# Attention bias tables loaded from ScalarE's queue in a two-layer streaming encoder

## The reference, cut to what matters

```python
x = x + 0.5 * swiglu(rmsnorm(x, g0), w_gu, w_down)
y = even_mixer(...) if l % 2 == 0 else odd_mixer(...)   # one layer each
x = x + y
x = x + 0.5 * swiglu(rmsnorm(x, g2), w_gu, w_down)
```

```python
s = einsum('bihd,bjhd->bhij', q, k) * D ** -0.5
s = s + bias                             # band: by distance, from a table
s = s + F_q[..., :, None] - F_k[..., None, :]   # fox: cumulative log forget values
p = softmax(s); o = einsum('bhij,bjhd->bihd', p, v)
```

## Time and profile before

| what | value |
|---|---|
| runs | 2955.0, 2948.9, 2955.4 us; median 2955.0 us |
| profiled execution | span of 2944.9 us from the first to the last instruction |
| TensorE matmul busy | 2773.1 us, 94% of the span |
| mean granted TensorE clock | 0.968 |
| VectorE, ScalarE, GpSimd busy | 25%, 24%, 32% |
| transfers | 293.49 MB, mean 100 GB/s |

### The profile page before, as it was taken

The page is one execution under the profiler, slowest core; times in us unless marked ns, Lnnn a source line. Parts: engine busy times, 40 slices in busy tenths (PEclk is TensorE's granted clock), DMA queues, the critical chain, the costliest instruction groups (busy, mean ns, idle before and its releaser), DMA issues.

```text
span 2944.9 us, 48416 instructions
## 1 busy us (share of the span) xinstructions
PE 2773.1 (94%) x19827; PEld 2646.2 (90%) x19827; DVE 739.6 (25%) x1751; ACT 708.7 (24%) x973; POOL 944.0 (32%) x285
## 2 busy tenths in 40 slices
PE   7999999999779999999999999999777789999997
PEld 7999999998548999999999999999545579999997
DVE  4110114323543211112211012311234433110112
ACT  2221222210242222122222122211244432221221
POOL 3443444330003344344344344432000013443442
PEclk9999999996699999999999999999899999999998
DMA  3212212112242221221221221222677832212211
GB/s 130 71 68 89 72 59 85 64 51 95 100 175 75 72 82 65 82 71 63 92 75 67 78 73 61 93 87 91 236 269 279 286 135 72 71 68 85 76 53 69
DMA packets 52873, 293.49 MB, mean 100 GB/s; under 512 B 8065, under 2 KB 11922, under 8 KB 28722
## 3 DMA queue, kind: packets, MB, share of 16 engines
q1 hardware_dynamic: 52786, 292.24, 28.1%
HBM read 279.95 MB, written 12.27 MB: 99 GB/s over the span
## 4 chain that ended last, share of the span: by engine, by line
PE 85%; DMA 5%; issue 4%; DVE 3%; ACT 1%; POOL 0%; SPq 0%; DVEq 0%; ACTq 0%
PE ps L306 75%; DMA s_bias<-neg_f_dram 4%; PE ps L670 4%; PE ps L932 1%; PE ps L984 0%; PE ps L922 0%; PE ps L1274 0%; DMA p_bias<-neg_f_dram 0%; DVE xn_lo L407 0%; PE ps L1263 0%; PE ps L372 0%; PE ps L1249 0%; PE ps L1269 0%; PE ps L912 0%; POOL w_lo L292 0%
## 5 line engine op out<-in xcount | busy, mean ns | idle before, releaser
L292 POOL TENSOR_TENSOR w_lo<-w_raw,w_hi 128x2048 fp32r<-128x2048 f32 (+2 forms) x185 | 791.7, 4279 | 1132.5 <-ACT w_hi L287 1124.2
L306 PE MATMUL ps<-xn_hi,w_hi 128*128 128x320 f32 x3616 | 829.8, 311 | 19.1 <-POOL w_lo L1641 10.9
L306 PE MATMUL ps<-xn_lo,w_hi 128*128 128x320 f32 x3616 | 827.4, 310 | 0.0
L306 PE MATMUL ps<-xn_hi,w_lo 128*128 128x320 f32 x3616 | 826.3, 310 | 0.0
L306 PEld LDWEIGHTS ps<-xn_hi,w_hi 128*128 128x128 f32 x3616 | 606.9, 189 | 21.6 <-POOL w_lo L1641 10.9
L306 PEld LDWEIGHTS ps<-xn_lo,w_hi 128*128 128x128 f32 x3616 | 607.8, 189 | 0.0
L306 PEld LDWEIGHTS ps<-xn_hi,w_lo 128*128 128x128 f32 x3616 | 607.6, 189 | 0.0
L287 ACT ACTIVATE w_hi<-w_raw 128x2048 fp32r<-128x2048 f32 (+2 forms) x185 | 326.6, 1766 | 533.5 <-PE ps L306 444.1
L559 POOL TENSOR_TENSOR h_lo<-prod,h_hi 128x640 f32 x88 | 139.1, 1581 | 716.5 <-ACT h_hi L512 716.5
L306 PE MATMUL ps<-h_hi,w_hi 128*128 128x320 f32 x1408 | 320.9, 309 | 0.0
L306 PE MATMUL ps<-h_hi,w_lo 128*128 128x320 f32 x1408 | 320.8, 309 | 0.0
(11 more groups left out here) (187 smaller groups left out, 2073.9 us busy)
## 6 DMA issues: line engine op xcount, KB each, us to landing
w_raw<-in_w_up SPq DMA_DIRECT2D x87, 1024.0 KB, 4.7
k_cache<-in_fox_kc SPq DMA_DIRECT2D x16, 2048.0 KB, 13.6
v_cache<-in_fox_vc SPq DMA_DIRECT2D x32, 1024.0 KB, 9.2
w_raw<-in_w_down_a SPq DMA_DIRECT2D x32, 768.0 KB, 4.3
w_raw<-in_w_in SPq DMA_DIRECT2D x24, 1024.0 KB, 4.7
w_raw<-in_w_down_b SPq DMA_DIRECT2D x32, 640.0 KB, 3.8
k_cache<-in_band_kc SPq DMA_DIRECT2D x8, 1024.0 KB, 7.0
v_cache<-in_band_vc SPq DMA_DIRECT2D x8, 1024.0 KB, 5.8
```

Of the source, the lines that this page charges most:

```text
L292: nc.gpsimd.tensor_tensor(out=w_lo[:, slot, 0:cols], in0=w_raw[:, slot, 0:cols], in1=w_hi[:, slot, 0:cols].bitcast(F32), op=ALU.subtract). ...
L306: last = nc.tensor.matmul(ps[:, 2 * unit + half, 0:HALF], w_part[:, slot, w:w + P], a_part[:, k, half * HALF:(half + 1) * HALF], start=k = ...
```

## The change

The bias loads of both stages are issued from ScalarE's queue. The pieces B (prompt bias, one head) and sB (sample bias, one unit) are put into ACT_HEAD and ACT_ORDER, each behind the exp that had to wait for the maximum that frees the tile, so they have no wait of their own. SyncE's order loses them with their waits; the rest of it is as it was. ScalarE waits for the end of GLA ahead of band. The data, the tiles and the semaphores that the loads raise are the same.

```diff
-    ACT_HEAD = "Q E0 E1 sE0".split()
+    ACT_HEAD = "sB0 B0 B1 Q E0 E1 sE0 sB1".split()
...
-    ACT_ORDER = ("C0 E2 sC0a sC0b sC0c C1 E3 C2 H0 E4 sE1 C3 E5 sH0 C4 H1 E6 sC1a sC1b sC1c C5 E7 Q+ C6 W H2 sE0+ "
-                 "C7 E0+ E1+ sH1 H3").split()
+    ACT_ORDER = ("C0 E2 sC0a sC0b sC0c C1 E3 C2 H0 E4 sE1 sB0+ C3 E5 sH0 C4 H1 E6 B0+ sC1a sC1b sC1c C5 E7 B1+ Q+ C6 W H2 "
+                 "sE0+ sB1+ C7 E0+ E1+ sH1 H3").split()
...
-                def bias(u):
-                    if not first or u:
-                        sp.wait_ge(self.smax_step, i * 4 + 2 * u)
-                    loads["bias"](i, u)
-
-                def prompt_bias():
-                    for hh in range(2):
-                        wait(self.max_step, i * 16 + (2 * hh - 2))
-                        sp.dma_start(p_bias[:, hh, :], self.prompt_bias(i, hh)).then_inc(self.bias_loaded[hh], 16)
...
+            def prompt_bias(i, hh):
+                act.dma_start(p_bias[:, hh, :], self.prompt_bias(i, hh)).then_inc(self.bias_loaded[hh], 16)
+
+            def sample_bias(i, u):
+                load_bias(i, u)
...
+    def fox_bias(act):
+        def load(i, u):
+            act.dma_start(s_bias[:, 0:PAST], after_dram[bass.ds(i * H_C + 8 * u, 8), :].unsqueeze(1)
+                          .broadcast_to([8, DEC_SEQ, PAST])).then_inc(fox.sbias_loaded[u], 16)
+            act.dma_start(s_bias[:, PAST:PAST + P], neg_f_dram[8 * u:8 * u + 8, SEQ:T].unsqueeze(1)
+                          .broadcast_to([8, DEC_SEQ, P])).then_inc(fox.sbias_loaded[u], 16)
+        return load
...
+                act.wait_ge(g_olo, H_A)
+                band.act(act, lambda: out_first(act, ph, band), band_bias(act))
...
+                fox.act(act, lambda: out_first(act, ph, fox), fox_bias(act))
```

More of the change, by code:

```diff
@@ L771, in out_dve @@
                 acc_dve(dve, s, u, (KT * r, SQ_STEPS * r))
-    PE_HEAD, DVE_HEAD, ACT_HEAD = "S0 S1 sS0".split(), "sQ0 sQ1 M0 M1 sM0".split(), "Q E0 E1 sE0".split()
+    PE_HEAD, DVE_HEAD, ACT_HEAD = "S0 S1 sS0".split(), "sQ0 sQ1 M0 M1 sM0".split(), "sB0 B0 B1 Q E0 E1 sE0 sB1".split()
     PE_ORDER = ("T0 S2 sT0a sT0b sT0c V0 sV0a T1 S3 V1 sV0b sS1 T2 X0 S4 V2 sV0c T3 S5 V3 sX0 T4 X1 S6 "
@@ L880, in body @@
                         space_free()
-                    bias(0)
-                    prompt_bias()
                     if not space_free:
@@ L888, in body @@
                     keys(1)
-                    bias(0)
                     value_chunk(0, 0)
-                    prompt_bias()
                     if self.chunks == 2:
                         value_chunk(0, 1)
-                bias(1)
                 for ch in range(self.chunks):
@@ L995, in pe, with act @@
             self.loop(pe, PE_HEAD, PE_ORDER, pieces)
-        def act(self, act, first_slab):
+        def act(self, act, first_slab, load_bias):
             parts = self.parts()
@@ L1042, in s_out_hi @@
                                          ACT.Copy).then_inc(self.sot_hi, 1)
-            pieces = dict(Q=queries, E=exps, C=copy_probs, H=out_hi, sE=s_exps, sC=s_copy_probs, sH=s_out_hi)
+            def prompt_bias(i, hh):
+                act.dma_start(p_bias[:, hh, :], self.prompt_bias(i, hh)).then_inc(self.bias_loaded[hh], 16)
+            def sample_bias(i, u):
+                load_bias(i, u)
+            pieces = dict(B=prompt_bias, sB=sample_bias, Q=queries, E=exps, C=copy_probs, H=out_hi, sE=s_exps, sC=s_copy_probs, sH=s_out_hi)
             pieces["W"] = lambda i: first_slab()
@@ L1160, in values, with band_bias @@
                          ).then_inc(band.sv_loaded[slot], 16)
[L1162 to L1166, removed]
+        return dict(keys=keys, values=values)
+    def band_bias(act):
+        def load(i, u):
+            act.dma_start(s_bias[:, 0:WIN + P], ins["band_bias_s"][bass.ds(i * 2 + u, 1)]
+                          .rearrange("o p c -> p (o c)")).then_inc(band.sbias_loaded[u], 16)
+        return load
     def fox_loads(sp):
@@ L1674, in _ @@
                 gla_act(act, ph)
-                band.act(act, lambda: out_first(act, ph, band))
+                act.wait_ge(g_olo, H_A)
+                band.act(act, lambda: out_first(act, ph, band), band_bias(act))
                 act.wait_ge(kv_even_stored, 32)
@@ L1681, in _ @@
                 act.wait_ge(logf_stored, 16)
-                fox.act(act, lambda: out_first(act, ph, fox))
+                fox.act(act, lambda: out_first(act, ph, fox), fox_bias(act))
                 act.wait_ge(kv_odd_stored, 48)
```

## The result

| | before | after |
|---|---|---|
| runs, us | 2948.9 to 2955.4, median 2953.6 (4) | 3008.9 to 3015.6, median 3015.2 (4) |
| ratio | | 1.0207, 95% interval 1.019 to 1.0225 |
| span of the profiled execution | 2944.9 | 3013.3 |
| mean granted clock | 0.968 | 0.956 |

The change makes the kernel 61.6 us slower. Forecast were 20 us, with 2998 as the upper end of the range. The sign was right, the size three times too small.

The account below looks back on a forecast made before the run. The prediction saw weight-stage matmuls carrying 79% of the span, largely out of the change's reach. Terms 16 + 4 - 2 + 2 = +20 us on span 2944.9, with the runs' 10.1 us offset, gave 2975; own range 2965 to 2990, wider range 2933 to 2998.

Parts of the forecast that it names:

- SyncE's issues removed: Both attention stages: taking the bias issues and waits off SyncE gains 0, as no later load hung on them.
- ScalarE's issue cost: Bias issues run under the exps in fox and band: 0 taken; fox bounds 0 and 13 us, band at most 2.
- Keys and values delayed: Fox passes: keys land later beside the bias but aren't waited for in the passes, so 0.
- Transfers in turn by row: Steady fox passes: two queues alternate row by row, so the sample bias add starts 2.3 us later; seven passes, +16 us.
- Until the first bias row moves: Fox pass: sample bias issued at 2199.39 was assumed to start moving at 2200.4, 1.0 us later.
- The 16 long rows: Fox pass, each of 8 engines: 12 of the 4 KB bias rows go beside keys until 2210.0, four after.
- Start of fox: First fox pass: prompt bias behind the sample bias, sharing engines with SyncE's loads; bounds +0 and +8 us, +4 taken.
- the second half of pass 0: First fox pass: its 2.3 us sample-bias stall falls away as the bias meets an empty queue, -2 us.
- Clock: Fox passes: two passes with TensorE's clock at 1.00 may join the others, 1.6 us each; +2 us taken.
- Rival 1: Fox passes: the sample bias overtakes the keys and the stalls go; -21 us, 2934 us; chance 0.30.
- Rival 2: Both queues drained one whole transfer at a time, so the time comes out the same, 2958 us; chance 0.20.
- Rival 3: Each change between queues costs an engine a fresh start; +40 us and up, 3000 to 3020 us; chance 0.08.

Follow-up runs that it names:

- after_keys1_waits: Changed kernel, but from the second fox pass SyncE issues the second half's keys only once the first half's sample bias has landed: 2945.8 us, ratio 0.9979.
- after_no_tail: Changed kernel with fox's 64 KB sample-bias transfer of 512-byte rows made only once, ahead of the first pass (later data stale): 2979.4 us, ratio 1.0090.
- after_keys_8k: Changed kernel with each 2 MB fox key load issued as two 1 MB transfers, rows 8 KB instead of 16 KB: 2996.0 us, ratio 1.0144.
- after_16_engines: Changed kernel with fox's sample bias read from 128 distinct values-cache rows, not 8 broadcast rows (same bytes, other data): 2937.1 us, ratio 0.9940.
- fox_prompt_only: Changed kernel with only fox's prompt bias issued from ScalarE's queue, all other bias loads left on SyncE's: 2964.8 us, ratio 1.0040 to the kernel before.
- band_only: Changed kernel with only band's two bias tables issued from ScalarE's queue, both of fox's left on SyncE's: 2956.0 us, ratio 1.0011 to the kernel before.
- keys1_behind_bias: Kernel before, all on SyncE's queue, with the sample bias issued ahead of the second half's keys in every pass but a stage's first: 2930.5 us, ratio 0.9923.

## Why the prediction was wrong, point by point

- SyncE's issues removed, 0: right. No load of SyncE's goes earlier to any use.
- ScalarE's issue cost, 0 (bounds 0 and 13): right in fox, by the timeline above and by after_keys1_waits. In band a small price: at its head ScalarE's `qz` starts at 779.7, not 778.4, behind the issues.
- Keys and values delayed, 0: right, though the keys take 16.0 us at the median to land, and not 13.6; no pass waits for them.
- **Transfers in turn by row, +2.3 us a pass, +16: the step that failed.** The mechanism held (after_no_tail, after_keys_8k, after_16_engines each change the number or the length of the turns, and the time follows), and its size was off. The stall grew by 6.7 us a pass, 47 in all. Counted in the pass of the timeline above, from the issue at 2223.60 to the add at 2246.59, the bias takes 23.0 us; the forecast had 18.0 (2199.39 to 2217.4). The parts, by the packet records of the trace:
  - Until the first bias row moves: 1.0 us forecast (2200.4), 4.1 measured. This is the larger half of the miss: I had let the bias start as if the engines were idle. In the seven passes it is 3.9 to 4.1 us, and where the engines are idle 1.4 us (the bias of the second half, issued at 2248.32). With 8 KB key rows it is 3.7 to 4.0 us as well, so it isn't a number of key rows that have to pass.
  - The 16 long rows: 11.6 us forecast (12 until 2210.0, 0.80 us a turn, which is the sum of both rows alone, and four turns of 0.5), 13.5 measured. A turn beside keys takes 0.92 us.
  - The 16 short rows, and 1 us to the add: 5.4 us forecast, 5.4 measured, and after_no_tail's 0.29 us a row agrees.

  Together that is 5.0 us later than I had it; the logits come 0.3 us later too, so the stall is 8.5 us and not 3.9.
  Also the prompt bias stood in no term of the passes: it has 16 rows an engine of its own, and fox_prompt_only puts its price, when it moves alone, at 2.8 us a pass by the profiled executions (1.5 of stall, the rest with the clock at 0.90); by the medians, 11.0 us in all, it is under 2.
  Queues of the kernel after in 2223.6 to 2227.6, after the issue beside keys, and in 2248.3 to 2249.7, after the issue into idle engines; q10 has no line in either:
```profile
DMA packets 109, 1.69 MB, mean 422 GB/s; under 512 B 4, under 2 KB 4, under 8 KB 4
...
q1 hardware_dynamic: 109, 1.69, 101.4%
```
```profile
DMA packets 0, 0.00 MB, mean 0 GB/s; under 512 B 0, under 2 KB 0, under 8 KB 0
```
- Start of fox, +4 (0 to +8): 7.2 us until the add of the second half, inside the bounds and near the turns that I had named and halved. In it, the second half of pass 0, for which I had -2, did lose its stall. It was the upper end that was right: the prompt bias is used 24.9 us after the first key load is issued, and 14.6 before. Band, for which I had 0 and 2 at most, delivers fox 4.4 us later. Its prompt bias is waited for 5.2 us, and not 2.3, and from its first query tile to its last sample add it takes 107.9 us, not 101.9 (107.8 in band_only; the median of that run, +2.2 us, has an interval of -1 to +7).
- Clock, +2: about 7 us of the passes (8.5 of longer matmuls). I had let two passes join the others at 0.95; all seven fell to 0.84 to 0.88, where TensorE stands still for 8 us in each and not for 2. A stall that grows was paid for a second time.

Rival 1 (the bias overtakes) fails with this transfer and holds with one that is spread over all engines. Rival 2 (whole transfers at a time) is refuted: it would have passes of 35 to 36 us. After the fact the Trainium skill's count of 9 to 17 descriptors for a packet (DMA: Bandwidth & Descriptors, "Queues, rings and completion order") doesn't describe these turns: taking away 16 short rows on each of 8 engines, some 8 KB of each, gave back 4.9 us a pass, and the 16 long rows of one engine lie spread over 13.5 us between key rows, not in one or two groups. Rival 3 (slower by much more) came to the right time, 3000 to 3020, and had 0.08; its cause was a fresh start at each switch, and the engines show none: their rows fill the time without gaps, and key rows are slower on engines that don't switch. What it had right is that a turn costs more than its two rows alone, and the range should have taken it in: the size of 2.3 us a pass rested on no row with two queues in it, nor did the 1.0 us to the first bias row.

The Trainium skill's rule that a second issuer saves only issue time (same page, "Issuing engines are not separate DMA queues") spoke against the change. The measured ratio of 1.0207 goes further: the order of issue in one queue is also a priority, and a second queue gives it up.

Open is what the first bias row waits for beside moving keys, and what makes the rows slower while the sample bias moves: its source, or its spread over 8 engines. A bias load that keeps its data and is spread over 16 engines wasn't tried.

## What to carry to other kernels

A queue is also an order: before you move a load to another queue, ask what its rows will alternate with until the last one has landed, and count rows on its busiest engine, not bytes. If a small load that is needed first lies behind a large one, put it ahead of it in the same queue (23 us here, 0.8%), and don't put it beside it (62 us, 2.1%, the other way). Where a trace doesn't show two queues at work together, give the wait for the first row a term of its own (4.1 us here, against 1.4 into idle engines), and take the sum of both rows alone as the lower bound of a turn, not the middle (here 0.80 us against 0.92).

## What the runs showed that I had not expected

- The first row of the bias moves 3.9 to 4.1 us after its issue beside key loads, and 1.4 us after it into idle engines.
- Key rows and broadcast bias rows together move 325 GB/s on a pair of queues, where keys alone move 412 to 442 and keys beside 128 distinct rows 395.
- 64 KB of 512-byte rows cost 4.9 us a pass on a second queue beside 8 and 16 KB rows, and 0.4 us behind their own bias in one queue.
- Moving the prompt bias alone cost 11 us, most of it in the passes, where nothing waits for it: it made the sample bias late. The load that is moved need not be the one whose wait grows.
- TensorE's granted clock was 0.84 to 0.88 in passes with one stall of 8 to 11 us, and 0.98 over the seven passes without a stall (after_keys1_waits, after_16_engines, keys1_behind_bias). Seven passes at 0.98 and without stalls take 239 us in the latter two, 5 more than the 234 that I had worked out as the floor, and 243 in the first.
